# A third set of value-page buffers in the memory of z's tiles, with z reloaded and gated late in the attention

## What is computed

```python
q, k, v, z, xbc, dt = _split_proj(u, w_in[i])
# prompt: two softmax maps per head, causal, 8 heads, blocks of 128 queries
o_attn = _attn_out(_prompt_diff_attn(q, k, v, lam), w_subln[i], lam_init)
...
# sample: 8 sequences, each with 2048 past tokens in 16 pages of 128
v_past = cache_v[i][page_table].reshape(db, past, N_ATTN_HEADS, DV)
o_attn = _attn_out(_sample_diff_attn(q, k, v, k_past, v_past, lam), w_subln[i], lam_init)
...
o_ssm = _ssm_out(y, xs, d_skip[i], z, w_ssm_norm[i])   # y is gated with z * sigmoid(z)
```

## Time and profile before

| | us |
|---|---|
| median of 3 runs | 2875.98 |
| lowest, highest | 2870.14, 2878.78 |
| the profiled execution | 2875.93 |
| its span in the profile | 2874.2 |
| PE busy | 2698.3 (94%) |
| DVE busy | 1335.4 (46%) |
| ACT busy | 777.9 (27%) |
| the 128 value-page transfers, of them each | 512 KB, 5.3 from issue to landing |

### The profile page before, as it was taken

The page is one execution under the profiler, slowest core; times in us unless marked ns, Lnnn a source line. Parts: engine busy times, 40 slices in busy tenths (PEclk is TensorE's granted clock), DMA queues, the critical chain, the costliest instruction groups (busy, mean ns, idle before and its releaser), DMA issues.

```text
span 2874.2 us, 50070 instructions
## 1 busy us (share of the span) xinstructions
PE 2698.3 (94%) x21661; PEld 2562.4 (89%) x21661; DVE 1335.4 (46%) x1501; ACT 777.9 (27%) x967; POOL 585.4 (20%) x290
## 2 busy tenths in 40 slices
PE   7999999957675999999999999999999999999998
PEld 7999999922244999999999999999999999999998
DVE  4277777628668423443333333333334333436433
ACT  3111111136743212322222222222222222223322
POOL 0098999200027001000000000001000000002322
PEclk9999999977876999999999999999999999999999
DMA  4388888398812322333333333323333333332333
GB/s 131 114 279 272 273 300 290 117 348 297 325 62 79 119 81 81 96 96 99 100 97 95 97 103 96 103 89 110 96 103 96 96 96 103 96 96 82 96 93 114
DMA packets 294895, 396.42 MB, mean 138 GB/s; under 512 B 14773, under 2 KB 256051, under 8 KB 292982
## 3 DMA queue, kind: packets, MB, share of 16 engines
q1 hardware_dynamic: 271688, 380.23, 40.7%
q10 hardware_dynamic: 22990, 13.01, 1.5%
HBM read 377.71 MB, written 15.58 MB: 137 GB/s over the span
## 4 chain that ended last, share of the span: by engine, by line
PE 78%; DVE 6%; POOL 5%; DMA 5%; issue 2%; SPq 2%; ACT 1%; ACTq 0%; DVEq 0%; POOLq 0%
PE ps L1171 25%; PE ps L1173 25%; PE ps L1176 25%; POOL kpage L1019 3%; DMA vpage<-in_cache_v 2%; DMA kpage<-in_cache_k 2%; PE ps L1271 1%; DVE wl L1646 1%; SPq L466 1%; POOL dl L1064 1%; PE ps L1534 1%; POOL bx L1072 1%; SPq L470 1%; DMA xs<-in_x_sample 0%; DVE hq L1861 0%
## 5 line engine op out<-in xcount | busy, mean ns | idle before, releaser
L1171 PE MATMUL ps<-uh,wh 128*128 128x260 f32 x4512 | 1184.9, 284 | 18.7 <-DVE wl L1646 13.4
L1173 PE MATMUL ps<-ul,wh 128*128 128x260 f32 x4512 | 1180.7, 283 | 0.0
L1646 DVE TENSOR_TENSOR wl<-raw,wh 128x1024 fp32r<-128x1024 f32 (+1 forms) x418 | 582.0, 1393 | 1247.0 <-ACT wh L602 1246.9
L602 ACT ACTIVATE wh<-raw 128x1024 fp32r<-128x1024 f32 (+1 forms) x418 | 441.0, 1056 | 1802.6 <-PE ps L1176 1750.7
L1176 PE MATMUL ps<-uh,wl 128*128 128x260 f32 x4512 | 907.9, 283 | 0.0
L1171 PEld LDWEIGHTS ps<-uh,wh 128*128 128x128 f32 x4512 | 853.3, 189 | 21.2 <-DVE wl L1646 10.9
L1173 PEld LDWEIGHTS ps<-ul,wh 128*128 128x128 f32 x4512 | 851.4, 189 | 0.0
L1176 PEld LDWEIGHTS ps<-uh,wl 128*128 128x128 f32 x4512 | 696.5, 189 | 0.0
L1171 PE MATMUL ps<-hh,wh 128*128 128x260 f32 x2048 | 536.5, 283 | 0.0
L1173 PE MATMUL ps<-hl,wh 128*128 128x260 f32 x2048 | 534.3, 282 | 0.0
L1176 PE MATMUL ps<-hh,wl 128*128 128x260 f32 x2048 | 410.6, 282 | 0.0
(11 more groups left out here) (333 smaller groups left out, 1511.0 us busy)
## 6 DMA issues: line engine op xcount, KB each, us to landing
kpage<-in_cache_k SPq DMA_DIRECT2D x128, 512.0 KB, 4.8
vpage<-in_cache_v SPq DMA_DIRECT2D x128, 512.0 KB, 5.3
raw<-in_w_up SPq DMA_DIRECT2D x128, 512.0 KB, 3.7
raw<-in_w_down SPq DMA_DIRECT2D x128, 512.0 KB, 3.4
raw<-in_w_in SPq DMA_DIRECT2D x88, 512.0 KB, 4.6
raw<-in_w_out SPq DMA_DIRECT2D x32, 512.0 KB, 3.5
raw<-in_w_ple_gate SPq DMA_DIRECT2D x32, 512.0 KB, 3.4
xt<-in_x_prompt SPq DMA_DIRECT2D x8, 1024.0 KB, 9.0
```

The lines of the kernel that those rows point to most:

```text
L602: A(wh[:, c % 2, 0:elems], raw[:, c % 2, 0:elems], ACT.Copy).then_inc(hi_ready, 1)
L1171: mm(ps[:, bank + 2 * m + f, 0:HALF], h_, xh[:, f * HALF:(f + 1) * HALF], start=st, stop=False)
L1173: mm(ps[:, bank + 2 * m + f, 0:HALF], h_, xl[:, f * HALF:(f + 1) * HALF], start=False, stop=False)
L1646: tt(wl[:, c % 2, 0:elems], raw[:, c % 2, 0:elems], wh[:, c % 2, 0:elems].bitcast(F32), ALU.subtract).then_inc(lo_ready, 1)
```

## The change

There is a third set of four page buffers, `vpage2`, in the 16 KB per partition that z's tiles take (16,640 bytes). Steps 0 to 3 and 28 to 31 use sets 0 and 1 in turn, and steps 4 to 27 use all three in turn, so that there the pages of step n may be issued when PE has finished step n - 3. Step 4 is the first in the new set and waits for the last copy of V's rows (`s_vto`), behind which the V tiles are free. z is reloaded after step 25, the last in the new set, ahead of page 28. z's sigmoids move to ACT's iterations 24, 26, 28 and 30, and its products to DVE's 25, 27, 29 and 31. The counter `s_vu` starts at 0 and no longer at 2, and its waits are written without the 2.

```diff
+        vpage = [sb("vpage0", [4, AW], F32, "XX"), sb("vpage1", [4, AW], F32, "RAW"),
+                 sb("vpage2", [4, AW], F32, "PJ", TZ * T * 4)]
+        V_SET = [0, 1, 0, 1] + [(n - 2) % 3 for n in range(4, 28)] + [0, 1, 0, 1]
+        V_TURN = [V_SET[:n].count(V_SET[n]) for n in range(4 * NB)]
...
-            def value_pages(u, i):
+            def value_pages(u, used, i):
...
-                    if j == 0:
-                        sp.wait_ge(s_vu, at(u + 1, 4, i))
-                    sp.dma_start(vpage[u % 2][:, j, :], d["cache_v"][0][bass.ds(idx, 1)]
-                                 .rearrange("o t h d -> (o t) (h d)")).then_inc(s_vp[u % 2], 16)
+                    if j == 0 and used is not None:
+                        sp.wait_ge(s_vu, at(used, 3, i))
+                    sp.dma_start(vpage[V_SET[u]][:, j, :], d["cache_v"][0][bass.ds(idx, 1)]
+                                 .rearrange("o t h d -> (o t) (h d)")).then_inc(s_vp[V_SET[u]], 16)
...
-            for u in range(3, 5):
-                value_pages(u, None)
+            value_pages(3, 2, None)
             sp.wait_ge(s_vto, NH)
+            value_pages(4, None, None)
             sp.dma_start(d_out["v_prompt"][0, 0].rearrange("(q p) h d -> p q (h d)", p=P), vtok)\
...
-            for u in range(5, 7):
-                value_pages(u, None)
+            value_pages(5, 3, None)
+            value_pages(6, 4, None)
+            with sp.Fori(0, 7) as i:
+                for u in range(7, 10):
+                    value_pages(u, u - 2, i)
+            sp.wait_ge(s_vu, 26)
             sp.wait_ge(s_zout, 16 * 5)
             sp.dma_start(pj[:, TZ:TZ + 8, :], z_scr.rearrange("t p n -> p t n")).then_inc(z_in, 16)
-            value_pages(7, None)
-            with sp.Fori(0, NB - 2) as i:
-                for u in range(8, 12):
-                    value_pages(u, i)
+            for u in range(28, 32):
+                value_pages(u, u - 1, None)
...
-                if s % 2 == 0 and 6 <= s < JOBS + 6:
+                if s % 2 == 0 and 6 <= s < CT + 6:
                     a_sigmoid(s - 6)
                     a_sigmoid(s - 5)
+                if s % 2 == 0 and 24 <= s < 32:
+                    a_sigmoid(CT + s - 24)
+                    a_sigmoid(CT + s - 23)
...
             def page_values(n):
 
                 pe.wait_ge(s_wz, n + 2)
-                pe.wait_ge(s_vp[n % 2], 64 * (n // 2 + 1))
+                pe.wait_ge(s_vp[V_SET[n]], 64 * (V_TURN[n] + 1))
...
-                if s % 2 and 7 <= s < JOBS + 7:
+                if s % 2 and 7 <= s < CT + 7:
                     silu(s - 7)
                     silu(s - 6)
+                if s % 2 and 25 <= s < 33:
+                    silu(CT + s - 25)
+                    silu(CT + s - 24)
```

More of the change, by code:

```diff
@@ L165, in build @@
         xsg = sb("xsg", [KT, NB], F32, "XX", 24576)
-        vpage = [sb("vpage0", [4, AW], F32, "XX"), sb("vpage1", [4, AW], F32, "RAW")]
+        vpage = [sb("vpage0", [4, AW], F32, "XX"), sb("vpage1", [4, AW], F32, "RAW"),
+                 sb("vpage2", [4, AW], F32, "PJ", TZ * T * 4)]
+        V_SET = [0, 1, 0, 1] + [(n - 2) % 3 for n in range(4, 28)] + [0, 1, 0, 1]
+        V_TURN = [V_SET[:n].count(V_SET[n]) for n in range(4 * NB)]
         se = sb("se", [3, 2, SEQ], F32, "XX", 20480)
@@ L308, in build @@
         s_dv, s_dp, s_dex = sem("dec_vector_steps"), sem("dec_tensor_steps"), sem("dec_exp")
-        s_vp = [sem(f"v_landed{i}") for i in range(2)]
+        s_vp = [sem(f"v_landed{i}") for i in range(3)]
         s_vu, s_wz = sem("v_used"), sem("page_weights_placed")
@@ L347, in build @@
         dec_squared_at = (5, 7)
-        z_in, g_y, z_y = sem("z_landed"), sem("dec_y_ready"), sem("gated")
+        z_in, z_y = sem("z_landed"), sem("gated")
         z_q, z_s, z_rt, z_o, z_h, z_l = (sem("gated_sq"), sem("gated_sum"), sem("gated_rms"),
@@ L461, in load_out @@
                 load(wcols(w_out, 512 * k, at(256 * g, 256, i)), c, 4, i)
-            def value_pages(u, i):
+            def value_pages(u, used, i):
                 for j in range(4):
-                    idx = sp.value_load(ptab[0:1, bass.ds(at(32 * j + u, 4, i), 1)], min_val=0,
+                    idx = sp.value_load(ptab[0:1, bass.ds(at(32 * j + u, 3, i), 1)], min_val=0,
                                         max_val=POOL - 1)
-                    if j == 0:
-                        sp.wait_ge(s_vu, at(u + 1, 4, i))
-                    sp.dma_start(vpage[u % 2][:, j, :], d["cache_v"][0][bass.ds(idx, 1)]
-                                 .rearrange("o t h d -> (o t) (h d)")).then_inc(s_vp[u % 2], 16)
+                    if j == 0 and used is not None:
+                        sp.wait_ge(s_vu, at(used, 3, i))
+                    sp.dma_start(vpage[V_SET[u]][:, j, :], d["cache_v"][0][bass.ds(idx, 1)]
+                                 .rearrange("o t h d -> (o t) (h d)")).then_inc(s_vp[V_SET[u]], 16)
             sp.wait_ge(s_kr, 4 + NB * PAGES)
-            value_pages(0, None)
+            value_pages(0, None, None)
             sp.wait_ge(w_used, SL_OUT + 2)
-            value_pages(1, None)
-            value_pages(2, None)
+            value_pages(1, None, None)
+            value_pages(2, 1, None)
             sp.wait_ge(s_kto, NH)
@@ L510, in _ @@
                 sp.dma_start(stt[:, t], src[t * P:(t + 1) * P]).then_inc(g_in[t], 16)
-            sp.wait_ge(s_vu, 2 + 4 * NB)
+            sp.wait_ge(s_vu, 4 * NB)
             for c in range(SL_OUT, SL_OUT + 4):
@@ L781, in _ @@
             act.wait_ge(g_bs, 16)
-            act.wait_ge(s_vu, 4 * NB + 2)
+            act.wait_ge(s_vu, 4 * NB)
             hi(SL_OUT)
@@ L1127, in _ @@
             pe.sem_inc(w_used, 2)
-            pe.sem_inc(s_vu, 2)
             pe.sem_inc(group_free, 2)
@@ L1271, in page_values @@
                         last = mm(ps[32 * j:32 * j + 32, 6 + f, :], zpad[:, n % 2, j, w0:w0 + 32],
-                                  vpage[n % 2][:, j, f * 512:(f + 1) * 512],
+                                  vpage[V_SET[n]][:, j, f * 512:(f + 1) * 512],
                                   start=False, stop=(n == 4 * NB - 1))
@@ L1822, in place @@
                 if n >= 2:
-                    dve.wait_ge(s_vu, 2 + n - 1)
+                    dve.wait_ge(s_vu, n - 1)
                 dve.tensor_copy(zpad[:, n % 2, :, 8:16], wd[:, n // PAGES:NB:2, n % PAGES, :]).then_inc(s_wz, 1)
@@ L1870, in dt_step @@
                 if k == 0:
+                    dve.wait_ge(s_zout, 16 * 5)
                     link(ts(X, dtt[0:NSH], hcol[0:NSH, 0:1], None, ALU.add))
@@ L1952, in _ @@
                 if s == 28:
-                    dve.wait_ge(s_vu, 2 + 4 * NB)
+                    dve.wait_ge(s_vu, 4 * NB)
                     dve.tensor_copy(oacc.rearrange("p (f n) -> p f n", f=2), ps[:, 6:8, :])\
```

## The result

The changed kernel takes 2855.21 us in the median of 4 runs (2853.29 to 2856.58), beside 2875.39 us for the kernel before (4 runs). The ratio is 0.9928 with a 95% interval of 0.9913 to 0.9944: 20 us or 0.7% faster. Run again in a later round it gave 2856.96 us beside 2874.23 us, ratio 0.9937 (0.9920 to 0.9954), 17 us.

The account below looks back on a forecast made before the run. The prediction took PE's attention as the bound, slowed by the two-set page loop, with DVE full in units 10 to 15. Terms 5.2 + 7.7 + 0 + 6.5 - 0.5 = 18.9 us off 2875.9 gave 2857 us, range 2850 to 2868.

Parts of the forecast that it names:

- z leaves the early queue: Early page steps: taking z's transfer out of the saturated queue brings step 7 forward by 5.2 us.
- Units 4 to 9 in 34 us: DVE's units 4 to 9: a third set cuts the stretch from 41.7 to 34 us, a gain of 7.7.
- the floor of 30.6 us: Units 4 to 9: six page steps at 5.1 us of transfer each; the forecast put 3.4 us on top.
- Units 10 to 15, nothing: DVE's units 10 to 15: DVE is full and its list unchanged, so nothing is gained, at most 1.5 us.
- Steps 22 to 31 in 54 us, gain 6.5: End of step 21 to end of step 31: 60.5 us before, 54 us with the third set and late z.
- Later gating: Iterations 28 to 31, behind the last page step: idle time covers most of the moved z work; 0.5 us is lost.
- PE's wait for pages: Sign in the new profile: PE's wait for value pages falls from 59.7 to under 30 us.
- the first rival: Page transfers: the queue does not hold 413 GB/s on pages alone, so 2864 us; chance 0.17.
- The second: Units 4 to 9 and 18 to 27: engine handovers set the pace, 2869.5 us, no change that can be told; chance 0.14.
- The third: Iteration 24: ACT stands still for z, making the kernel slower if z takes 38 us to land; chance 0.03.

Follow-up runs that it names:

- z late and two sets: The changed kernel with the third set taken away, z still reloaded and gated late: 2875.46 us, ratio 1.0005 to the kernel before.
- the half pages: Half of each value page loaded, read twice by PE: 2840.4 us on the changed kernel (three sets), 2848.9 us on the kernel before (two sets).

## Why the prediction was right

The forecast was 2857 us and it measured 2855.2 and 2857.0. The mechanism was right: two sets lose time in the loop of page step, issue and landing, and a third set gives it back. That the sum came so close is in part luck, since single terms are off by up to 3 us, in both directions. By the steps of the sum:

- **z leaves the early queue, 5.2 us.** Right, and about the right size: with two sets it brings step 7 4.5 us forward, with the spread of 1.6 us named above. In the changed kernel step 7 is 6.5 and 5.1 us earlier and unit 4 8.4 and 6.9 us. I take the rest to belong to the third set, as page 7 no longer has to wait for step 5; I had counted that only from unit 4 on.
- **Units 4 to 9 in 34 us.** Measured 33.9 and 32.3, in four executions with full pages and dt in its old place 32.3 to 33.9. The number is right, the reason for its last 3.4 us is not shown. I had taken them for handover between the engines, on top of the floor of 30.6 us. But the page steps ran at the floor: the six steps from 8 to 14 took 30.2 and 30.1 us. And the list of what could set the pace (DMA, DVE, ACT and PE) lacked SP, whose issues take 4.9 us a step, just under the 5.1 of the bytes. The stretch itself is measured between two starts of DVE, and it is longer because unit 4 starts 2.7 us ahead of step 8 and unit 10 1.0 us behind step 14 (2.0 and 0.2 us in the other execution, 0.0 and 0.2 before the change).
- **Units 10 to 15, nothing.** Measured 1.1 us slower, 50.4 after 49.4, in every kernel with pages in time and the old list, and not with z late and two sets. In unit 10 DVE waits 0.98 us for ACT's tap in both executions of the changed kernel, a wait that the kernel before did not have.
- **Steps 22 to 31 in 54 us, gain 6.5.** Measured 55.3 and 56.9, a gain of 5.3 and 3.7. The fault is in the sentence on z, that it stands ahead of page 28 while PE works on pages 26 and 27. These did not cover it: step 28 waited 3.65 us for its pages, the last of which landed 10.1 us after its issue.
- **Later gating, -0.5 us.** The term is small, as forecast, but its place was wrong. I had put it in unit 31; there nothing shows. In the first execution it was 1.2 us in unit 27, which I had not looked at, since a pair of products and a head's reciprocal now meet in it; in the second it was nothing. From unit 28 to unit 31 the first execution also takes 21.7 us, as in six of the eight runs with z late, and the second 20.8, as before the change; why is not shown.

One of the signs that I named did not come: PE's wait for pages fell to 37.0 us and not under 30. The waits of steps 2, 3 and 5, which the change leaves nearly as they were, make up 18.0 us of it, and that of step 28 3.65.

The rivals: the queue did hold its rate, 415 GB/s for 34 us of pages alone, so the first rival did not happen. The Trainium skill's page "HBM Reference", section "Specifications (TRN2)", gives some 358 GB/s as a core's share, and more for a core that streams alone; with the second part this trace agrees, at 415 GB/s. The second, that handovers fill the place of the page waits, did not happen at its size: units 4 to 9 became 7.8 and 9.5 us shorter. What the engines need there without any page wait stays open, as the half pages still had such waits. The third did not happen in the changed kernel, but it is near: with z one page later ACT waits 2.9 us, and the queue behind z costs more than that.

From step 0 to unit 31 the changed kernel is 19.2 and 20.6 us shorter; the sum was 18.9. What lies ahead of step 0 differs by up to 5.8 us between the executions of all these kernels, and what lies behind unit 31 by up to 2.6, in both directions, and I have no cause for it. So the spans differ by this much beside what the attention wins.

## What to carry to other kernels

Where a wait on a transfer and a wait on a free buffer release each other in turn, write down the loop: work, issue, landing, over the number of sets. If it is longer than the bytes alone would take, a further set or a shorter way to the landing helps, until the next bound is reached. Count the issuing engine among those bounds: here its issues took 4.9 us a step beside 5.1 us for the bytes. Half the bytes test the transfers but not the issues, so look at what is still waited for before you read such a run as the pace of the others. A large reload in the same queue cost about the same here early and late, so look at what is queued behind it. And once transfers are on time, look in the stretch with a full engine for work that nobody needs yet: here that gave 7 to 9 us more.

## What the runs showed of the hardware

One core held 415 GB/s into its memory for 34 us from transfers of 512 KB, each row 4 KB, at a DMA share of 1.03; I had seen 413 only with stores mixed in. The same list of instructions of PE, DVE and ACT took 32.3 to 33.9 us in that stretch, and 32.5 when the DMA engines were busy 0.7 of the time, with SP issuing at the same pace. SP took 1.24 us from one page issue to the next, each with a read of the page table, over 31 issues without a wait for PE. And the clock that PE was granted in units 4 to 9 was 0.75 before and 0.90 after: of the page steps 8 to 13 three took about 3.64 us before, and one after, the others 1.9 to 2.0.
